# Two-block transformer on one core: ScalarE squares and finishes the layer norm ahead of the first mixer, in place in X

## The reference, cut to what matters

```python
def layer_norm(x, g, b):
    mu = jnp.mean(xf, axis=-1, keepdims=True)
    var = jnp.mean(jnp.square(xf - mu), axis=-1, keepdims=True)
    y = (xf - mu) * lax.rsqrt(var + LN_EPS) * g + b
...
x = layer_norm(DEEPNORM_ALPHA * x + swiglu(x, ...), ln_g[l, 1], ln_b[l, 1])   # l = 1: the end of block one
...
h = jnp.concatenate([meta, x], axis=1)
h = h + hybrid_mixer(rmsnorm(h, norm_mix_g[0]), w_in[0], ...)
```

## Time and profile before

| what | us |
|---|---|
| median of 3 runs (2634.19 to 2636.61) | 2634.43 |
| the profiled execution, its own time | 2636.31 |
| its span in the trace | 2634.4 |
| PE busy | 2596.0 (99%) |
| DVE busy | 1359.3 (52%) |
| ACT busy | 1038.9 (39%) |

### The profile page before, as it was taken

One profiled execution on the slowest core, in us unless ns is written; L12 is line 12 of the kernel. 1 busy time (PEld: TensorE's weight loads), 2 busy tenths in 40 slices (PEclk: granted clock), 3 DMA queues, 4 the chain that ended last, 5 costly groups with the idle time before them and its releaser, 6 DMA issues.

```text
span 2634.4 us, 42702 instructions
## 1 busy us (share of the span) xinstructions
PE 2596.0 (99%) x18898; PEld 2321.8 (88%) x18898; DVE 1359.3 (52%) x2196; ACT 1038.9 (39%) x1700; POOL 40.2 (2%) x90
## 2 busy tenths in 40 slices
PE   9999999999999999999999999999999999999998
PEld 7777888888887788888899899999999989999998
DVE  6766533324656543333567446555336754655533
ACT  4554422213545442221455344344224534543421
POOL 0000000000100000000000000000000000000000
PEclk9999999999999999999999999999999999999999
DMA  5221222222312122222231222222223113222222
GB/s 189 88 67 62 82 95 96 92 99 81 110 64 79 65 96 96 96 90 88 95 103 51 74 91 95 83 95 93 89 90 124 66 58 105 90 88 97 93 89 76
DMA packets 39865, 235.75 MB, mean 89 GB/s; under 512 B 5520, under 2 KB 7824, under 8 KB 17536
## 3 DMA queue, kind: packets, MB, share of 16 engines
q1 hardware_dynamic: 34912, 214.45, 23.9%
q0 software_dynamic: 4048, 17.00, 2.0%
q10 hardware_dynamic: 720, 1.57, 0.2%
HBM read 222.38 MB, written 6.42 MB: 87 GB/s over the span
## 4 chain that ended last, share of the span: by engine, by line
PE 94%; DVE 3%; ACT 2%; DMA 0%; issue 0%; SPq 0%; DVEq 0%; ACTq 0%
PE P L535 78%; PE P L627 3%; PE P L649 3%; PE P L542 2%; PE P L661 1%; PE P L885 1%; DVE WL L1809 1%; PE P L675 1%; PE P L998 1%; PE P L906 1%; PE P L707 1%; ACT WH L1245 0%; PE P L1048 0%; DVE X L1941 0%; DMA X<-in_xT 0%; PE P L1050 0%
## 5 line engine op out<-in xcount | busy, mean ns | idle before, releaser
L535 PE MATMUL P<-XH,WL 128*128 128x264 f32 (+3 forms) x3080 | 844.2, 323 | 17.1 <-DVE XL L1958 6.0
L535 PE MATMUL P<-XL,WH 128*128 128x264 f32 (+3 forms) x3080 | 823.0, 316 | 0.0
L535 PE MATMUL P<-XH,WH 128*128 128x264 f32 (+3 forms) x3080 | 820.5, 315 | 0.0
L1809 DVE TENSOR_TENSOR WL<-raw,WH 128x1024 fp32r<-128x1024 f32 (+1 forms) x403 | 482.6, 1201 | 529.4 <-ACT WH L1245 528.8
L1245 ACT ACTIVATE WH<-raw 128x1024 fp32r<-128x1024 f32 (+1 forms) x403 | 417.3, 1039 | 597.8 <-PE P L535 595.6
L535 PEld LDWEIGHTS P<-XH,WL 128*128 128x128 f32 x3080 | 520.4, 188 | 66.6 <-DVE XL L1958 8.0
L535 PEld LDWEIGHTS P<-XH,WH 128*128 128x128 f32 x3080 | 519.0, 189 | 37.9
L535 PEld LDWEIGHTS P<-XL,WH 128*128 128x128 f32 x3080 | 518.8, 188 | 36.8
L2479 DVE SCALAR_TENSOR_TENSOR tmp<-P,PP,tmp 128x527 f32<-128x527 f32 (+1 forms) x88 | 66.8, 759 | 195.3 <-ACT tmp L1754 195.3
L535 PE MATMUL P<-GHH,WL 128*128 128x264 f32 (+1 forms) x704 | 149.1, 283 | 0.0
L535 PE MATMUL P<-GHL,WH 128*128 128x264 f32 (+1 forms) x704 | 148.9, 282 | 0.0
(11 more groups left out here) (344 smaller groups left out, 3414.2 us busy)
## 6 DMA issues: line engine op xcount, KB each, us to landing
raw<-in_wts SPq DMA_DIRECT2D x169, 1024.0 KB, 4.9
raw<-in_wts SPq DMA_DIRECT2D x32, 896.0 KB, 4.6
spill<-X POOLq DMA_DIRECT2D x2, 2112.0 KB, 9.3
X<-spill POOLq DMA_DIRECT2D x16, 264.0 KB, 3.0
qswap<-qraw SPq DMA_DIRECT2D x44, 64.0 KB, 2.0
tab<-in_tR POOLq DMA_DIRECT2D x2, 1056.0 KB, 5.3
tmp<-in_biasT POOLq DMA_DIRECT2D x16, 128.0 KB, 3.2
tmp<-in_biasT POOLq DMA_DIRECT2D x16, 112.0 KB, 2.7
```

The lines of the kernel that those rows point to most:

```text
L535: ins = nc.tensor.matmul(P[:, a:a + x1 - x0], wb[:, s, 128 * k:128 * k + 128], xb[:, kx, x0 - c0:x1 - c0], start=start and i == 0, stop=st ...
L1809: nc.vector.tensor_tensor(WL[:, u % NS, 0:length(u)], raw[:, u // 2 % RAW, a:a + length(u)], WH[:, u % NS, 0:length(u)].bitcast(F), ALU.su ...
```

## The change

Only the norm s = 3 is touched. DVE's `normal` writes its product in place in X, and `result` is gone from DVE. ACT squares straight from that product, with gain and bias as scale and bias of the ACTIVATE (`gain`: each a pointer to one value for each partition), and later makes the result itself, in place in X (`gained`, event xf). The squares of the 16 meta tokens, once part of the 264 tokens of half 0, are three ACTIVATEs of their own (one for slots 0 to 5, then one each for tiles 6 and 7). The orders change as well: on DVE, `centre` of half 1 moves from ahead of the RMS norm of half 0 to between its tiles (`beside`, two centred tiles after each of m = 3 to 6). On ACT, the squares of half 1 come after high parts 4 to 7. On PE, the eight sums of half 0 come in one piece ahead of mean(1); all eight sums of half 1's variance stand in phase 0 after k = 4 to 7; the RMS sums of half 1 stand in phase 1 after k = 5 and k = 7.

```diff
                 if s == 3:
-                    sums(0, 0, 1, 2, 3)
+                    sums(0, *range(8))
                     mean(1)
-                    sums(0, 4, 5, 6, 7)
-                    var(1, 0, 1, 2, 3)
...
-                        if phase == 0 and k in (1, 2):
-                            var(1, 2 * k + 2, 2 * k + 3)
-                        elif phase == 1 and k % 4 == 3:
-                            sums(1, *range(k - 3, k + 1))
+                        if phase == 0 and k >= 4:
+                            var(1, 2 * k - 8, 2 * k - 7)
+                        elif phase == 1 and k in (5, 7):
+                            sums(1, *range(2 * k - 10, 2 * k - 6))
...
                     for m in range(8):
-                        square_again(s, m, 0)
-                        if m == 4:
-                            highs(top + 2)
-                    for m in range(4):
-                        square(m, 1)
+                        square_again(l, s, m, 0)
+                    highs(top + 2)
+                    for m in range(3):
+                        gained(l, s, m, 0)
                     root_again(s, 0)
                     for m in range(8):
+                        if m < 5:
+                            gained(l, s, m + 3, 0)
                         feed(s, m, 0)
-                        if m < 2:
-                            square(2 * m + 4, 1)
-                            square(2 * m + 5, 1)
+                        if m >= 4:
+                            square(2 * m - 8, 1)
+                            square(2 * m - 7, 1)
                         elif m == 3:
                             highs(top + 3)
-                        elif m == 4:
-                            root(1)
+                    root(1)
                     for m in range(8):
-                        square_again(s, m, 1)
+                        square_again(l, s, m, 1)
+                    for m in range(3):
+                        gained(l, s, m, 1)
                     root_again(s, 1)
                     for m in range(8):
+                        if m < 5:
+                            gained(l, s, m + 3, 1)
                         feed(s, m, 1)
...
+            def gain(l, m):
+                return {"scale": par("ln_g", 16 * l + 8 + m), "bias": par("ln_b", 16 * l + 8 + m)}
...
+                act.wait_ge(*at("nrm", s, m, hf))
+                nc.scalar.activation(SQ[:, m % 6, a:b], X[:, m, a:b], ACT.Square, **gain(l, m)).then_inc(*act.up("xsq", s, m, hf))
+
+            def gained(l, s, m, hf):
+                a, b = HV[hf]
+                nc.scalar.activation(X[:, m, a:b], X[:, m, a:b], ACT.Identity, **gain(l, m)).then_inc(*act.up("xf", s, m, hf))
...
                     for m in range(8):
                         normal(m, 0)
-                        result(m, 0)
-                        if m == 4:
-                            res(7, 1)
+                    res(7, 1)
                     lows(top + 2)
-                    centre(1, *range(8))
                     g0 = pc["nmix"]
-                    rms_half(s, g0, 0)
+                    rms_half(s, g0, 0, lambda m: centre(1, 2 * m - 6, 2 * m - 5) if 3 <= m < 7 else None)
                     lows(top + 3)
                     for m in range(8):
                         normal(m, 1)
-                        result(m, 1)
```

More of the change, by code:

```diff
@@ L1400, in layer_norm, with square_again @@
                     result(m, 1)
[L1402 to L1406, removed]
+            def gain(l, m):
+                return {"scale": par("ln_g", 16 * l + 8 + m), "bias": par("ln_b", 16 * l + 8 + m)}
+            def square_again(l, s, m, hf):
+                a, b = HV[hf]
                 if m >= 6:
                     act.wait_ge(*at("ms", s, m - 6, hf))
-                nc.scalar.activation(SQ[:, m % 6, a:b], X[:, m, a:b], ACT.Square).then_inc(*act.up("xsq", s, m, hf))
+                if not hf and m in (0, 6, 7):
+                    n = 6 if m == 0 else 1
+                    act.wait_ge(meta_loaded, 16)
+                    nc.scalar.activation(SQ[:, m % 6:m % 6 + n, 0:META], X[:, m:m + n, 0:META], ACT.Square).then_inc(*act.up("msq", s, m))
+                act.wait_ge(*at("nrm", s, m, hf))
+                nc.scalar.activation(SQ[:, m % 6, a:b], X[:, m, a:b], ACT.Square, **gain(l, m)).then_inc(*act.up("xsq", s, m, hf))
+            def gained(l, s, m, hf):
+                a, b = HV[hf]
+                nc.scalar.activation(X[:, m, a:b], X[:, m, a:b], ACT.Identity, **gain(l, m)).then_inc(*act.up("xf", s, m, hf))
             def root_again(s, hf):
@@ L1946, in normal @@
                     dve.wait_ge(*at("rsl", s, hf))
-                    if m >= 4:
-                        dve.wait_ge(*(at("xf", s, m - 4, hf) if s == 3 else at("xl", ver, m - 4, hf)))
                     if s == 3:
-                        nc.vector.tensor_tensor(tmp[m % 4][:, a:b], X[:, m, a:b], rstd[:, a:b], ALU.mult).then_inc(*dve.up("nrm", s, m, hf))
+                        nc.vector.tensor_tensor(X[:, m, a:b], X[:, m, a:b], rstd[:, a:b], ALU.mult).then_inc(*dve.up("nrm", s, m, hf))
                     else:
+                        if m >= 4:
+                            dve.wait_ge(*at("xl", ver, m - 4, hf))
                         nc.vector.scalar_tensor_tensor(tmp[m % 4][:, a:b], X[:, m, a:b], par("ln_g", p0 + m), rstd[:, a:b], ALU.mult, ALU.mult
@@ L1959, in split @@
                                                    ALU.add, ALU.subtract).then_inc(*dve.up("xl", ver, m, hf))
[L1961 to L1966, removed]
                 for m in range(8 - last, 8):
@@ L2013, in rms_half @@
                         dve.wait_ge(*at("rstd", s, hf))
+                        if s == 3:
+                            dve.wait_ge(*at("xf", s, m, hf))
                         if m >= 4 and s < 7:
@@ L2022, in rms_half @@
                                                 ).then_inc(*dve.up("xl", s + 1, m - 2, hf))
-                    if m == 3 and beside:
-                        beside()
+                    if beside:
+                        beside(m)
             def feed_forward(l):
@@ L2198, in res, with beside @@
                     nc.vector.tensor_tensor(X[:, m, a:b], X[:, m, a:b], P[:, o:o + b - a], ALU.add).then_inc(*dve.up("res", s, m, hf))
[L2200 to L2203, removed]
+                def beside(m):
+                    if m == 3:
+                        if last == 1:
+                            lows(top + 2)
+                        res(7, 1)
                 for m in range(8 - last, 8):
```

## The result

The changed kernel takes 2644.72 us (median of six runs, 2641.60 to 2645.18), the kernel before 2636.38 (six runs, 2634.19 to 2636.99): ratio 1.0028, with a 95% interval of 1.0019 to 1.0038, that is 5.0 to 10.0 us slower (the quotient of the two medians is 1.0032, a difference of 8.3 us). The profiled execution took 2645.07, with a span of 2643.3. The page's shares look as in the earlier trace rows: DVE is relieved by 6.1 us, ACT loaded with 9.2, and PE is busy for 3.0 us more with the same 18898 instructions. Work that takes longer at an equal count points to the clock, and the rest of the loss, 5.9 of the 8.9 us by which the spans differ, must be idle time of PE.

A forecast was written before the change was run, and what follows sets the result against it. It took two chains ending in a Ln, and PE's work between them, as the bound. 4.0 + 0.95 + 0.25 + 0.2 + 1.7 = +7.1 on the median 2634.43 gave 2641.5 us, range 2638.0 to 2644.2.

The forecast's parts named there:

- free pointers: Bound on ACT's squares and results: scale and bias by pointer cost nothing, waits sum to +4.0.
- the last rival: First Ln's 1.7 gain kept, no pointer cost, no 1.2 GHz stretch behind the second pause: -1.4, 2633.0; chance 0.03.
- Bank wait: Head of phase 0: PE waits for bank 4 until half 1's last tile is centred, starting at 1301.0, +4.0.
- Clock: Head of phase 0: new 1.2 GHz stretch after PE's 8.5 us pause, +1.7, from nothing to twice that.
- The rival with a full clock: Head of phase 0: clock doesn't fall again or recovers before PE restarts; +5.4, 2639.8; chance 0.25.
- Four sums in phase 0 and squares with pointers: Phase 0 to second Ln: four more sums on PE, half 1's squares slower at 0.51 each; +0.95.
- three results: Ahead of the second Ln: ACT still has three results to make, since its squares ended late; +0.25.
- the stream of half 1: After the second Ln: five tiles at ACT's 0.84 for result and high part, against DVE's 0.75; +0.2.
- Pointers: ACT's squares: scale and bias by pointer add 181 ns; a square takes 0.59, one going each 0.50.
- The first Ln: Half 0's RMS norm on ACT: Ln starts at 1292.55, 1.7 earlier than before.
- Late copy of X: Behind the norm: X's copy issued +11.9 later delays a weight load and ACT's high part; 2645.6; chance 0.08.
- The bank wait does not bind: Head of phase 0: PE starts with the first low part at 1295.3; +1.8, 2636.2; chance 0.07.

The follow-up runs named there:

- e1: Changed kernel, but PE takes only banks 0 to 3 ahead of phase 0 and banks 4 and 5 ahead of phase 1; ratio 1.0004.
- e5: Kernel before, with PE's first matmul of phase 0 waiting for the fifth tile's low part instead of the first; 2641.12 us, ratio 1.0016.
- e3: Changed kernel plus 16 matmuls of constants into a free bank, filling PE's pause ahead of phase 0; ratio 1.0016.
- e4: Changed kernel with this layer norm's gain and bias left out, so ACT works without pointers; ratio 1.0029.
- e7: Kernel before plus only ACT's takeover of squares and results with pointers, orders as before except two places; ratio 0.9999.
- e9: Kernel before, unchanged, profiled in one more execution; not timed, 34.82 us from the 16 variance passes to half 1.

## Why the prediction came out right, point by point

It gave 2641.5 with 2638.0 to 2644.2, slower. The median is 2644.72, by 8.3 above that of before. Taken by itself that median lies 0.5 above the range; but the forecast was built on 2634.43, the median of three runs of before, and the six runs here gave 2636.38. As a difference the range was +3.6 to +9.8, and 8.3 lies in it; the recorded ratio applied to 2634.43 gives 2641.8. The stage grew by 7.46 where the sum said 7.1. The direction and the two mechanisms were right, sizes were off in both directions, and it is partly luck that the sum came so close: the wait came out 0.3 below its term, the clock 0.9 above, the rest 0.2 below.

Three numbers of the prediction do not follow from its own working, and none of them decides anything. The range is 0.4 wider on either side than the bounds that were added up (+4.0 to +9.4); free pointers take 1.4 off the waits (5.4 to 4.0), not 1.5; and with 1.4 the last rival is 2633.1. The terms:

- **Bank wait, predicted +4.0: right in kind, 3.7 in size.** The wait is ended by L1953. e1 takes it away and the stage falls by 5.75; e5 puts a delay of 3.22 into the kernel before and the stage grows by 5.93. From the origin, phase 0 starts 3.71 later. At 1302.09 less the shift of 1.36 that is 1300.73; 1301.0 was predicted.
- **Clock, predicted +1.7: right in kind, too small; 2.6 measured (e3).** I had taken half of the stretch seen behind 2.7 us of pause. The stretch behind the 8 us pause was longer, and so long that it covered 5.7 us of work although it had begun within the pause. This is the term that was mis-sized: 2.6 within bounds of 0 and 3.4. Nor does the length of the pause fix it: in e4, behind a nearly equal pause of 7.53, the clock was back after 3.3 us of work, and the way to the first group of sums took only 1.5 longer than in e3 (5.22 against 3.76), where in the changed kernel it took 2.5 longer (6.30). The rival with a full clock (2639.8) is what e3 runs: its 2642.41 against 2636.87 is +5.5, as the 5.4 of that case.
- **Four sums in phase 0 and squares with pointers, +0.95; three results, +0.25; the stream of half 1, +0.2: together 1.4, measured 1.19 (e3).** The last term did not come: from the second Ln to PE's matmul it was 2.67 and is 2.65, and to the table load the changed kernel is 7.48 later, no more than to half 1. In e7, at full clock, the gain of 0.34 at half 1 is still 0.32 at the table load of e9. The three results cost almost nothing either: ACT was through with them at 1321.39, PE with its last sum at 1321.19, and the Ln began at 1321.30.
- **Pointers.** A square takes 0.58 to 0.60, six go each 0.49, as predicted from (792 - 611): a difference between forms of 528 tokens held for 248. Two meta squares of 16 tokens took 0.21 and 0.20, the next instruction beginning 0.12 and 0.10 later; I had taken 0.16. The sentence on the Trainium skill, "ScalarE: Activation LUTs", section "What ACT_TABLE_LOAD costs", gave an estimate of 0.20 and 0.11: by that rule, the trace agrees.
- **The first Ln** came 1.9 earlier (1.7 predicted), half of the difference because the two meta squares went each 0.11 and not 0.16.
- **Late copy of X, a rival at 0.08: it came, and cost nothing.** The copy's issue moved from 1311.45 to 1326.43, 13.6 later by the origin. ACT then did wait for the weights (POOL's row, ACT's row, and the landing times of the two weight loads issued from 1333.69 on):

```profile
1326.43 0.59 POOL L494 DMA_DIRECT2D spill<-X  x1 [513.32 <-ACT X L1421]
```

```profile
1342.57 1.07 ACT L1243 ACTIVATE WH<-raw 128x1024 fp32r<-128x1024 f32 x1 [0.97 <-DMA raw<-in_wts]
DMA to landing us min/median/max: 5.2/7.0/8.9
```

  But the high part is not what PE needs next: the result ahead of it, at 1340.98 (before 1332.15), is 7.47 later than before by the origin, the amount of the stage, and the difference of the spans is 8.9 = 7.46 + 1.36 and 0.1. The wait of 0.97 stayed off the path. The page cited there, the Trainium skill, "Trainium Kernel Development and Optimization", section "Key Constraints", has queues interleave on the same engines. The trace fits that as far as it goes. The load was issued where the stage put it, at 1333.69 in place of 1324.86, and took 8.9 us to land in place of the 5.9 of the earlier trace rows; so it was slowed, not issued late. The copy itself took 7.7 and had landed by 1334.2; what shared the time with the load was what POOL had queued behind the copy, above all a load of 1056 KB that took 8.7 in place of 5.3.
- **"The bank wait does not bind", 2636.2: refuted by the trace, and built by e1.** There the start is free and the stage 1.71 longer, for the 1.8 at which this rival was priced (near by luck: the start was 0.2 earlier than its sum had it, and the wait of 0.42 ahead of phase 1 was not in it); its period of 1.43 a tile and its 2.1 for three waits were measured at 1.42 to 1.43 and 2.02.

What stays open: the timed difference (8.3 by medians, 5.0 to 10.0) is above the stage's 7.46 by an amount that falls within the interval; stretches of low clock elsewhere, which come and go between executions, are enough for it: the one at the head of half 1 is worth 1.4 (43.21 against 41.79), and the longer one near 200 us moved the origin by 1.3. And e4's time lies 7.3 above before where its stage says 5.5; it, too, is within its interval.

## What to carry to other kernels

Look for every resource that one wait takes in a lump, and ask for each when it comes free in the new order: here bank 4, which no matmul writes before phase 1 (48 matmuls of products and the eight sums of phase 0 stand ahead of it), cost more than the work saved. Price a longer pause of TensorE as its own length plus half the time of the work that then runs at 1.2 GHz; here a delay of 3.2 us cost 5.9 in the stage. And measure such a change by the distance between two fixed instructions of the trace as well as by the device time: stages repeated within 0.02 us where the clock kept its level (34.80 and 34.82, 34.46 and 34.44, 34.82 and 34.80), while times spread by more than 2 us.

## What the runs showed of the hardware that was not expected

- The length of the low stretch was not fixed. At 1.2 GHz PE worked 3.4 us behind the pause of 2.71, 5.7 behind 4.58 (e5), 5.7 behind 7.99, where the clock had already fallen within the pause, and only 3.3 behind 7.53 (e4).
- Behind nearly equal pauses of 2.70 to 2.77 us it fell in seven executions of eleven, and for the same kernel (before) in one of two. Behind 4.55, 4.58, 7.53, 7.98 and 7.99 it fell each time.
- The length of the pause alone does not decide. Behind pauses of 1.08 (e3), 1.36 and 2.37 (e1, ahead of phase 0) the clock stayed full, but a pause of 2.05 near 198 us went with a fall in eleven executions of fourteen.
